# Feed-forward gate and up products: the input's low and main parts as one moving operand of 512 columns

## The reference, cut to what matters

```python
hn = rms_norm(h, norm2_g)
ffn = (jax.nn.silu(hn @ w_gate) * (hn @ w_up)) @ w_down     # w_gate, w_up: 1024 x 2816, w_down: 2816 x 1024
return h + ffn
```

## Time and profile before

| | |
|---|---|
| time, median of 3 runs | 1293.5 us (1293.47 to 1295.22) |
| the profiled execution's own time | 1294.48 us |
| its span from first to last instruction | 1292.5 us |
| mean granted clock of TensorE | 0.975 of full |
| PE / PEld / DVE / ACT / POOL busy | 92 / 66 / 52 / 47 / 60 % of the span |
| share of the chain that ended last: L738 / L1018 / L1274 | PE 28 / 18 / 4 % |

### The profile page before, as it was taken

How to read it: one execution, slowest core, us unless ns; L and a number is a source line. 1 busy time by engine, 2 the same in 40 slices (tenths; PEclk the granted TensorE clock), 3 DMA queues, 4 the chain that set the end, 5 groups by cost and what they waited for, 6 DMA issues and landing times.

```text
span 1292.5 us, 16299 instructions
## 1 busy us (share of the span) xinstructions
PE 1187.4 (92%) x6168; PEld 853.5 (66%) x6168; DVE 672.9 (52%) x1463; ACT 603.6 (47%) x1318; POOL 779.4 (60%) x487
## 2 busy tenths in 40 slices
PE   8999999999987778788798788889999999999998
PEld 8987999975332333233354344433889999999998
DVE  5433144279776675867758677655554233311112
ACT  7486564534323232234425544453755655544442
POOL 7796668745555454544444453453276668788885
PEclk9999999999999988989999899989999999999999
DMA  8453447989999999999999999999534436555542
GB/s 267 161 164 117 145 159 244 317 349 406 426 426 425 426 425 426 426 425 426 424 426 425 425 426 426 424 396 388 197 124 137 131 131 196 166 194 190 178 154 98
DMA packets 129150, 381.82 MB, mean 295 GB/s; under 512 B 8496, under 2 KB 81200, under 8 KB 96304
## 3 DMA queue, kind: packets, MB, share of 16 engines
q0 software_dynamic: 36864, 268.45, 49.6%
q1 hardware_dynamic: 90736, 112.25, 26.5%
q10 hardware_dynamic: 1472, 0.09, 0.1%
HBM read 379.72 MB, written 1.05 MB: 295 GB/s over the span
## 4 chain that ended last, share of the span: by engine, by line
PE 68%; DMA 18%; DVE 8%; ACT 3%; issue 2%; POOL 1%; another core or an unknown queue 0%; SPq 0%; DVEq 0%; ACTq 0%
PE ps L738 28%; PE ps L1018 18%; DMA rows_w<-peer_rows_in,arena 11%; DMA arena<-peer_rows_in,arena 6%; PE ps L761 6%; PE ps L1274 4%; DVE rows_w L2461 2%; PE ps L1227 2%; DVE arena L2461 2%; PE ps L1083 1%; PE ps L1104 1%; ACT wgt L1586 1%; ACT diag L1595 1%; POOL arena L697 1%; PE ps L936 1%
## 5 line engine op out<-in xcount | busy, mean ns | idle before, releaser
L504 POOL TENSOR_TENSOR w_lo<-ring,w_hi 128x1024 fp32r<-128x1024 f32 x184 | 445.6, 2439 | 172.5 <-ACT w_hi L498 172.3
L1018 PE MATMUL ps<-rows_w,diag 128*128 128x512 f32 x500 | 247.6, 627 | 61.6 <-ACT diag L1595 61.6
L697 POOL DMA_INDIRECT rows_w<-peer_rows_in,arena x126 | 149.5, 1186 | 175.3 <-PE ps L1018 153.8
L498 ACT ACTIVATE w_hi<-ring 128x1024 fp32r<-128x1024 f32 x184 | 189.6, 1058 | 129.0 <-PE ps L738 90.8
L1018 PE MATMUL ps<-arena,diag 128*128 128x512 f32 x436 | 217.0, 639 | 31.7 <-ACT diag L1595 31.7
L1018 PEld LDWEIGHTS ps<-rows_w,diag 128*128 128x128 f32 x500 | 94.9, 198 | 190.8 <-issue 101.7
L697 POOL DMA_INDIRECT arena<-peer_rows_in,arena x109 | 134.6, 1235 | 134.0 <-PE ps L1018 104.0
L738 PE MATMUL ps<-hT_hi,w_hi 128*128 128x256 f32 x704 | 201.2, 286 | 0.0
L738 PE MATMUL ps<-hT_lo,w_hi 128*128 128x256 f32 x704 | 199.2, 283 | 0.0
L738 PE MATMUL ps<-hT_hi,w_lo 128*128 128x256 f32 x704 | 199.2, 283 | 0.0
L2461 DVE CUSTOM_DVE_ANT_0 rows_w<-rows_w,arena 128x1024 f32<-128x1024 f32 x126 | 153.0, 1223 | 80.6 <-DMA rows_w<-peer_rows_in,arena 80.0
(11 more groups left out here) (457 smaller groups left out, 1877.5 us busy)
## 6 DMA issues: line engine op xcount, KB each, us to landing
ring<-w_in_in SPq DMA_DIRECT2D x40, 1024.0 KB, 5.2
ring<-w_ffn_gate_in SPq DMA_DIRECT2D x11, 1024.0 KB, 5.4
ring<-w_ffn_up_in SPq DMA_DIRECT2D x11, 1024.0 KB, 5.2
ring<-w_ffn_down_in SPq DMA_DIRECT2D x11, 1024.0 KB, 5.0
ring<-w_out_in SPq DMA_DIRECT2D x8, 1024.0 KB, 6.5
ring<-w_branch_attn_in SPq DMA_DIRECT2D x4, 1024.0 KB, 5.1
ring<-w_branch_mlstm_in SPq DMA_DIRECT2D x4, 1024.0 KB, 5.4
ring<-peer_w_query_in SPq DMA_DIRECT2D x4, 1024.0 KB, 8.4
```

The lines of the kernel that those rows point to most:

```text
L498: act.activation(hi_of(n, u)[:, t, 0:cols], raw_half(n, g)[:, t, 0:cols], ACT.Copy).then_inc(sem("hi_ready"), 1)
L504: pool.tensor_tensor(lo_of(n, u)[:, t, 0:cols], raw_half(n, g)[:, t, 0:cols], hi_of(n, u)[:, t, 0:cols].bitcast(F32), ALU.subtract).then_i ...
L697: pool.indirect_dma_start(pick_row(p, 0, 2 * D), None, a["peer_rows"], bass.IndirectOffsetOnAxis(ap=idx[:, g // PH, j:j + 1], axis=0)).the ...
L1018: ins = pe.matmul(acc[:, c, :], diag[:, p % 4, :], pick_row(p, D + c * CW, CW), start=(p == first), stop=True, skip_group_check=True)
```

## The change: what it does

The two input tiles become one, `hT` = [low, main] with 2 x 8 x 256 elements; `hT_lo` and `hT_hi` are its halves, at the addresses that they had. A new helper `split_pair` takes `split_half`'s place in the feed-forward loop alone. For each input tile t and feature group j it issues two products in place of three: W_hi by [x_lo | x_hi], 512 columns into a whole bank, whose moving operand is two runs of 256 elements that lie 2048 elements apart, and W_lo by x_hi, 256 columns into the bank's upper half. A half now takes two banks (gate 0 and 1, up 2 and 3), and each bank holds two sums, by x_lo and by x_hi, which DVE has to add.

So DVE does three operations where it did one for the gate (scale the low sum into the new SBUF area `by_low`, scale the main sum in place, add), and three where it did one for the up half; the first add of each needs the operation before it to be finished, which `link` waits for. Since all four banks now belong to one chunk, PE waits at each half from chunk 1 on: the gate half of chunk c for `gate_scaled` of chunk c-1, and the up half for `hid_ready` of chunk c-1. The number of semaphores' increments and the down products stay as they are.

```diff
--- before.py
+++ after.py
@@ -137,10 +137,9 @@
         xres = sb("xres", [P, NB, D])
         with ExitStack() as shared:
             xn = shared.enter_context(nc.sbuf_tensor("xn", [P, NB, D], F32))
-        hT_lo = sb("hT_lo", [P, KT, S], R32)
-        with ExitStack() as shared:
             x3t = shared.enter_context(nc.sbuf_tensor("x3t", [P, KT, S], F32))
-        hT_hi = sb("hT_hi", [P, KT, S], R32)
+        hT = sb("hT", [P, 2, KT, S], R32)
+        hT_lo, hT_hi = hT[:, 0], hT[:, 1]
         with ExitStack() as shared:
             arena_r = shared.enter_context(nc.sbuf_tensor("arena_r", [P, 23808], R32))
         arena = sb("arena", [P, 23808])
@@ -315,6 +314,8 @@
         hidden = Area(3072 + 1024)
         hid_hi = hidden.take(4, 2, S, dt=R32)
         hid_lo = hidden.take(4, 2, S, dt=R32)
+        by_low = hidden.take(2, S)
+        gate_low, gate_main, up_low, up_main = [ps[:, first:first + 2, e * S:(e + 1) * S] for first in (0, 2) for e in range(2)]
         mask_str = sb("mask_str", [P, P])
         tri = sb("tri", [P, P])
         lev_mask = sb("lev_mask", [P, len(LEVELS) - 1, P])
@@ -739,6 +740,21 @@
                                                 skip_group_check=True)
                     ins.then_inc(sem("unit_used"), 1)
 
+            def split_pair(n, g, fresh=None):
+
+                for u, ts, _ in split_units(n, g):
+                    pe.wait_ge(sem("lo_ready"), u + 1)
+                    hi, lo = hi_of(n, u), lo_of(n, u)
+                    for t in range(ts.start, ts.stop):
+                        if fresh is not None:
+                            pe.wait_ge(sem("in_low"), fresh + max(t + 1, 2))
+                        for j in range(2):
+                            js = slice(j * P, (j + 1) * P)
+                            bank = ps[:, 2 * g + j, :]
+                            pe.matmul(bank.rearrange("p (e s) -> p e s", e=2), hi[:, t, js], hT[:, :, t, :], start=(t == 0), stop=(t == KT - 1), skip_group_check=True)
+                            ins = pe.matmul(bank[:, S:2 * S], lo[:, t, js], hT_hi[:, t, :], start=False, stop=(t == KT - 1), skip_group_check=True)
+                    ins.then_inc(sem("unit_used"), 1)
+
             banks = [None, None]
 
             def split_wide(n, g, evac, first, apart=0, fresh=None):
@@ -1276,10 +1292,10 @@
                     ins.then_inc(sem("unit_used"), 1)
 
             for c, n in enumerate(ffn_chunk):
-                if c >= 2:
-                    pe.wait_ge(sem("hid_ready"), c - 1)
                 for g in range(2):
-                    split_half(n, g, False, ps[:, (2 * c + g) % 4, :], fresh=None if c or g else LOW_X4)
+                    if c:
+                        pe.wait_ge(sem("hid_ready" if g else "gate_scaled"), c)
+                    split_pair(n, g, fresh=None if c or g else LOW_X4)
                     if c == 0 and g == 1:
                         pe.wait_ge(sem("r4_ready"), 1)
                         pe.wait_ge(sem("in_low"), LOW_X4 + 2)
@@ -1899,7 +1915,7 @@
                 act.wait_ge(sem("hid_sum"), c + 1)
                 if c >= 4:
                     act.wait_ge(sem("unit_used"), unit[down_half[c - 4]] + 2)
-                act.activation(hid_hi[:, c % 4, :, :], ps[:, (2 * c + 1) % 4, :].rearrange("p (a b) -> p a b", a=2), ACT.Copy).then_inc(sem("hid_hi"), 1)
+                act.activation(hid_hi[:, c % 4, :, :], up_main, ACT.Copy).then_inc(sem("hid_hi"), 1)
 
             c = 0
             for i, (n, g) in enumerate(ffn_halves):
@@ -2616,14 +2632,17 @@
             for c in range(NFF):
                 dve.wait_ge(sem("unit_used"), ffn_unit[c] + 2)
                 x = silu[:, c % 2, :, :]
-                up = ps[:, (2 * c + 1) % 4, :].rearrange("p (a b) -> p a b", a=2)
-                dve.tensor_tensor(x, ps[:, (2 * c) % 4, :].rearrange("p (a b) -> p a b", a=2), rbc.unsqueeze(1).broadcast_to([P, 2, S]),
-                                  ALU.mult).then_inc(sem("gate_scaled"), 1)
+                scale = rbc.unsqueeze(1).broadcast_to([P, 2, S])
+                dve.tensor_tensor(by_low, gate_low, scale, ALU.mult)
+                link(dve.tensor_tensor(gate_main, gate_main, scale, ALU.mult))
+                dve.tensor_tensor(x, gate_main, by_low, ALU.add).then_inc(sem("gate_scaled"), 1)
                 dve.wait_ge(sem("unit_used"), ffn_unit[c] + 4)
                 dve.wait_ge(sem("silu_ready"), c + 1)
-                dve.tensor_tensor(up, x, up, ALU.mult).then_inc(sem("hid_sum"), 1)
+                dve.tensor_tensor(by_low, up_low, x, ALU.mult)
+                link(dve.tensor_tensor(up_main, up_main, x, ALU.mult))
+                dve.tensor_tensor(up_main, up_main, by_low, ALU.add).then_inc(sem("hid_sum"), 1)
                 dve.wait_ge(sem("hid_hi"), c + 1)
-                dve.tensor_tensor(hid_lo[:, c % 4, :, :], up, hid_hi[:, c % 4, :, :].bitcast(F32), ALU.subtract).then_inc(sem("hid_ready"), 1)
+                dve.tensor_tensor(hid_lo[:, c % 4, :, :], up_main, hid_hi[:, c % 4, :, :].bitcast(F32), ALU.subtract).then_inc(sem("hid_ready"), 1)
             for b in range(NB):
                 for e in range(2):
                     es = slice(e * CW, (e + 1) * CW)
```

## The result

The changed kernel takes 1296.7 us (median of 20 runs, 1295.5 to 1301.2) against 1293.5 of the kernel before: ratio 1.0025, 95% interval 1.0019 to 1.0031. That is 3.2 us slower (2.5 to 4.0). The forecast was 1293.9 and "no measurable change" at 0.77. The time lies in the range for 8 in 10 (1291.7 to 1297.5), but above the forecast's own range, which ended at 1296.0. I had put 0.16 on this side.

The account below looks back on a forecast made before the run. PE was taken as the bound. Against the profiled execution, +2.97 us for chunk 1's start, -4.03 for products behind it and +1.5 for the clock gave +0.4; put on the median, 1293.9, range for 8 in 10 1291.7 to 1297.5.

Parts of the forecast that it names:

- What bounds the kernel: Last stage, from 1102.11 us to VectorE's last step: PE is the bound, without a hole.
- Part 1, the products: Feed-forward products: three of 256 become one of 512 and one of 256, saving 0.0126 us a triple, 4.4 us over 352.
- Part 2, DVE's steps: DVE after each half: 2.03 us where one operation took 0.69; 29 us more work, free unless PE waits.
- Part 3, steady state: Later chunks: DVE and ACT chains stay hidden behind PE's products, with 2.1 us spare for the up half.
- E: Steady state: DVE's chain is later than 5.5 us, each further us costing up to 10 times; chance 0.03.
- Part 4, the hole: Start of chunk 1: PE waits 3.37 us for DVE's gate scaling, starting 2.97 us later than before.
- D: Whole kernel faster, 1289 to 1290 us: the hole is hidden or the merge wins more; chance 0.06.
- Part 5, the clock: Behind the hole at chunk 1: TensorE's granted clock falls to 0.50, costing 1.5 us, from 0 to 3.1.
- B: Rival at the hole: the clock stays at 1.00, giving -1.1 us, or 1292.4; chance 0.28.
- A: The forecast as summed, with hole, products' gain and clock fall: 1293.9 us, own range 1292.8 to 1296.0; chance 0.50.
- the prediction's own sign: Whole kernel: the forecast would be wrong if the time moved by more than 2.6 us.
- C: Rival, slower: the merged product misses the 512-column pace, through its two runs or fixed part; 1298.4 at 0.240 us; chance 0.11.

Follow-up runs that it names:

- e1: Changed kernel, but the feed-forward low and main parts lie side by side, so the 512-column moving operand is one run; ratio 1.0023 to the kernel before.
- e8: e4 with each unit's products ordered two of 512 columns, then two of 256; one run, stage 184.74 us against 188.57 in the kernel before.
- e2: Changed kernel's banks, waits and DVE steps, but three products of 256 columns as before; ratio 1.0037 to the kernel before.
- e4: Changed kernel, but chunk 0 in its old form and gate and up banks swapped, so chunk 1's gate half waits for nobody; ratio 0.9975 to before.
- e7: Changed kernel with 20 tiny fills added to DVE's list after chunk 5, shifting its later program; ratio 1.0012 to the kernel before.
- e6: Changed kernel with 14 idle products of 128 columns in PE's list while it waits for DVE before chunk 1; ratio 1.0012 to before.

## Why the prediction was right or wrong

- **What bounds the kernel** (PE, in one piece): right. Every gain and loss shown above is PE time or the tail behind the end of PE.
- **Part 1, the products: right in kind, mis-sized.** The term was 0.0126 a triple, 4.4 us in all. Chunk 0 won its 0.40 as forecast (0.42 from the stage's begin to the first small product), but behind the down products a triple won 0.0067, so the whole won about 2.4 instead of 4.4. The bound from the earlier trace rows pointed at two runs, which e1 cleared. What I left out is that all rows of before are streams of one width. The 12.6 ns are real (e8 reaches 0.348), but 512 and 256 in turn keep them only in some stretches. The rule of the Trainium skill (TensorE: Matmul & The Clock Gate, Back-to-back issue gap) would have had 0.0025; neither order agrees with it.
- **Part 2, DVE's steps:** right: 1113.63 to 1115.67 is 2.04 us for three, forecast 2.03.
- **Part 3, steady state:** right. One wait in eleven chunks, and e2's cycle equals that of before to 0.01. E is out.
- **Part 4, the hole:** right: 3.37 us forecast, 3.37 measured (3.34 more than before); chunk 1 starts 2.94 later relative to the stage's begin, forecast 2.97. D is out. e4 shows it from the other side.
- **Part 5, the clock:** right in kind. In all four profiles with an open hole it fell (changed, e1, e2, e7), which makes B the less likely case; 1.5 was the size of the short falls (1.4 to 1.5 from e1 and e2), and the profiled execution had the long one, 2.7 by the difference to e6. In these four traces a fall that began 0.4 to 0.5 us behind PE's restart lasted 3.4 us, and one that began 0.9 to 1.0 ahead of it 6.8.
- **Not in the forecast at all: the tail.** "The order and number of SP's transfers stay" was true, yet the last one lands 1.1 us later. The step that failed is the silent one, that a longer DVE program costs only its run time.

The sum with the measured terms, for the profiled execution's stage and tail: 2.94 - 320 x 0.0067 + 2.7 + 1.16 = +4.7, against 3.50 + 1.16 = 4.66 shown. For the median, 2.94 - 320 x 0.0067 + 1.1 + (0 to 2.7) = +1.9 to +4.6, with 3.2 measured. A short fall of 1.4 to 1.5 fits within the interval, but no run here shows how the clock went in the executions that were not profiled. So A's mechanism held, and 2 us of products and 1.1 of tail lifted it from nothing to a small loss. "No measurable change" was wrong by the prediction's own sign. That 1296.7 still lies in the wide range owes something to luck: two terms missed to the slow side, and the 1298.4 of C is nearer to it than A's 1293.9. C is half of what happened: its loss of the products' gain came in part (a merged product of 0.353 - 0.120 = 0.233, just under its limit of 0.2335), though not for its reasons. The chances had a slip too: the parts named for "slower" add up to 0.18, not 0.16.

## What to carry to other kernels

A merge of products must be priced at the pace of the mix that it makes, not of streams of one width, and read in more than one stretch. Where it leaves two widths, pairs or groups of each held the better pace in every stretch here. A change that takes the second buffer away must be walked through at its first use, where the producer of a one-time operand may be late: here one late factor cost more than 320 triples won, and keeping the old form for the first chunk alone turned 3.2 us slower into 3.2 faster (with 1.1 of it from the last store). Where a hole stays, filling it with idle products keeps the clock, but count their records first.

## What was not expected of the hardware

- Fp32r products of 512 and 256 columns issued in turn have two paces: 0.347 us a pair in chunk 0 of the changed kernel, 0.353 behind down products; in pairs of each it is 0.348 throughout. Whether the 512 columns are one run or two makes no difference (cycles of 33.51 both).
- Where an 8 KB packet of the instruction queue fell into the last store, the store landed after 3.2 us in place of 2.0; 20 more instructions ahead in DVE's list removed that.
- A hole of 3.4 us in otherwise dense work dropped the granted clock to 0.50 in four of four profiles, for 3.4 or 6.8 us (1.4 to 1.5, or 2.7 us of loss); 14 idle products in it kept the clock at 1.00.
